# Turning rows into columns by block transposes and DRAM: a network's inner rows on ScalarE's queue, and two branches and half a convolution taken off TensorE

## Time and profile before

| | |
|---|---|
| median of 3 runs | 891.3 us |
| the profiled execution | 890.65 us, its span 888.9 us |
| mean granted clock of TensorE | 0.997 |
| TensorE, VectorE, ScalarE busy | 99%, 71%, 52% of the span |
| mean DMA rate | 242 GB/s |

### The profile page before, as it was taken

The page is one execution under the profiler, slowest core; times in us unless marked ns, Lnnn a source line. Parts: engine busy times, 40 slices in busy tenths (PEclk is TensorE's granted clock), DMA queues, the critical chain, the costliest instruction groups (busy, mean ns, idle before and its releaser), DMA issues.

```text
span 888.9 us, 11084 instructions
## 1 busy us (share of the span) xinstructions
PE 878.5 (99%) x4079; PEld 732.8 (82%) x4079; DVE 631.6 (71%) x883; ACT 460.7 (52%) x697; POOL 40.8 (5%) x66
## 2 busy tenths in 40 slices
PE   9999999999999999999999999999999999999996
PEld 7878888888998888888888888888888888888885
DVE  6769987837558877688578886875768766665743
ACT  6546554626688475446535554454445344444530
POOL 0010000022103000000000000001000100000000
PEclk9999999999999999999999999999999999999998
DMA  9899999774654454454699999975755577777741
GB/s 365 346 323 352 359 363 351 270 237 145 182 175 175 162 193 164 149 186 143 218 308 348 344 329 323 333 257 163 257 179 177 182 248 241 240 233 246 250 120 47
DMA packets 94879, 215.12 MB, mean 242 GB/s; under 512 B 14520, under 2 KB 46185, under 8 KB 94697
## 3 DMA queue, kind: packets, MB, share of 16 engines
q1 hardware_dynamic: 94104, 212.97, 69.8%
q10 hardware_dynamic: 720, 1.44, 0.4%
HBM read 204.66 MB, written 9.72 MB: 241 GB/s over the span
## 4 chain that ended last, share of the span: by engine, by line
PE 94%; DMA 2%; DVE 1%; issue 1%; ACT 1%; SPq 0%; POOL 0%; POOLq 0%; DVEq 0%
PE ps L741 29%; PE ps L743 29%; PE ps L742 29%; DMA t_raw<-in_f_up 2%; PE ps L679 1%; PE ps L656 1%; PE ps L649 1%; PE ps L858 1%; PE ps L874 1%; PE ps L816 0%; PE ps L850 0%; PE ps L798 0%; DVE t_wl L1209 0%; DMA t_acc<-in_xT 0%; PE ps L865 0%
## 5 line engine op out<-in xcount | busy, mean ns | idle before, releaser
L1209 DVE TENSOR_TENSOR t_wl<-t_raw,t_wh 128x1024 fp32r<-128x1024 f32 (+3 forms) x308 | 360.4, 1203 | 103.3 <-ACT t_wh L916 102.4
L916 ACT ACTIVATE t_wh<-t_raw 128x1024 fp32r<-128x1024 f32 (+3 forms) x308 | 307.8, 1040 | 106.9 <-DMA t_raw<-in_f_up 63.3
L741 PE MATMUL ps<-t_wh,t_XH 128*128 128x512 f32 (+2 forms) x640 | 250.2, 391 | 1.3 <-DVE t_wl L1209 1.3
L743 PE MATMUL ps<-t_wh,t_XL 128*128 128x512 f32 (+2 forms) x640 | 247.1, 386 | 0.0
L742 PE MATMUL ps<-t_wl,t_XH 128*128 128x512 f32 (+2 forms) x640 | 246.8, 386 | 0.0
L741 PEld LDWEIGHTS ps<-t_wh,t_XH 128*128 128x128 f32 x640 | 120.2, 188 | 24.8 <-DVE t_wl L1209 2.1
L743 PEld LDWEIGHTS ps<-t_wh,t_XL 128*128 128x128 f32 x640 | 120.1, 188 | 24.0
L742 PEld LDWEIGHTS ps<-t_wl,t_XH 128*128 128x128 f32 x640 | 120.3, 188 | 22.9
L741 PE MATMUL ps<-t_wh,t_YH 128*128 128x512 f32 x288 | 113.1, 393 | 0.2 <-DVE t_YL L1634 0.2
L743 PE MATMUL ps<-t_wh,t_YL 128*128 128x512 f32 x288 | 112.2, 390 | 0.0
L742 PE MATMUL ps<-t_wl,t_YH 128*128 128x512 f32 x288 | 112.2, 389 | 0.0
(11 more groups left out here) (225 smaller groups left out, 614.1 us busy)
## 6 DMA issues: line engine op xcount, KB each, us to landing
t_raw<-in_f_up SPq DMA_DIRECT2D x130, 512.0 KB, 5.6
t_raw<-in_f_dn SPq DMA_DIRECT2D x66, 512.0 KB, 5.5
t_raw<-in_ada SPq DMA_DIRECT2D x48, 512.0 KB, 6.3
inner_rows<-t_tp SPq DMA_DIRECT2D x60, 128.0 KB, 3.8
t_tp<-inner_rows SPq DMA_DIRECT2D x15, 512.0 KB, 5.2
t_raw<-in_mkv SPq DMA_DIRECT2D x8, 512.0 KB, 3.6
t_raw<-in_ga SPq DMA_DIRECT2D x8, 512.0 KB, 3.3
t_raw<-in_gc SPq DMA_DIRECT2D x8, 512.0 KB, 3.2
```

Source lines behind the costliest of these rows:

```text
L741: pe.matmul(o, xh, h, start=k == 0, stop=False)
L743: x = pe.matmul(o, xl, h, start=False, stop=k == n - 1)
L916: act.activation(wh[:, m % SPL, lo:w], raw[:, n % RAW, lo:w], ACT.Copy).then_inc(hi_made, 1)
L1209: dve.tensor_tensor(wl[:, n % RAW, lo:w], raw[:, n % RAW, lo:w], wh[:, m % SPL, lo:w].bitcast(F32), ALU.subtract).then_inc(drained, 1)
```

## The change

1. The nets' `spill` and `reload` move from SyncE's list to ScalarE's, with the same transfers. Their places are later: `ways` goes from (3, 4, 6) to (3, 5, 7) for the first of the first net, from (0, 1, 3) to (1, 2, 3) for the fifth of each net, and from (0, 1, 4) to (2, 4, 6) for the rest.
2. Branches c and a go by block transposes and DRAM (`blocks`, `spill`, `reload`, `y_in`), with SyncE's queue and two further buffers, the halves of `acc2`. Branch b keeps TensorE's way. `load_cond(1)` moves from unit 41 to 57 of the mixing block, since `cond` is one of these buffers.
3. Half 0 of the convolution goes the same way, `u` through `tp` and the gate through half of `acc2`. `cT` has four rows of 512 in place of two, so that half 0's taps stay there. Its gate product (`gate_in`) comes in the first unit of `conv_gb1`, its low parts (`gate_low` 0,0 and 0,1) in the last. Half 1 keeps TensorE's way.

```diff
-            ways = (3, 4, 6) if (f, q) == ("f1", 0) else (0, 1, 3 if q == 4 else 4)
+            ways = (3, 5, 7) if (f, q) == ("f1", 0) else (1, 2, 3) if q == 4 else (2, 4, 6)
...
+    for n, br in ((36, "c"), (39, "a")):
+        for m, step in ((0, "blocks"), (1, "spill"), (3, "reload"), (6, "y_in")):
+            side[n + m] = side.get(n + m, []) + [(step, br)]
...
-                unit("conv_cc1", m, *([("gate_turn", 0, m), ("gate_low", 0, m)] if m < 2 else []))
+                unit("conv_cc1", m, *([], [("ut_in",), ("spill", "gb")], [("conv_taps", 0, 0)], [("reload", "gb"), ("conv_taps", 0, 1)])[m])
...
-        for m, steps in enumerate(([("conv_turn", i, 0), ("conv_turn", i, 1)], [("conv_taps", i, 0)], [("conv_taps", i, 1)], [])):
+        if i == 0:
+            S.append(("blocks", "uu"))
+            turns = [], [("spill", "uu")], [], [("reload", "uu")]
+        else:
+            turns = ([("conv_turn", i, 0), ("conv_turn", i, 1), ("gate_in",)], [("conv_taps", i, 0)], [("conv_taps", i, 1)],
+                     [("gate_low", 0, 0), ("gate_low", 0, 1)])
+        for m, steps in enumerate(turns):
             unit(f"conv_gb{i}", m, *steps, ahead=5 + (i and m // 2))
         S.append(("conv_gb", i))
+        if i == 0:
+            S.append(("blocks", "gb"))
...
-            cT = sb("cT", [P, 2, 512], F32, c)
+            cT = sb("cT", [P, 4, 512], F32, c)
...
+        way = tp, acc2[:, 1, :], acc2[:, 0, :]
...
+        def way_out(q, key):
+            n, w = way_width(*key), way_of(*key)
+            q.wait_ge(*blocked.at(*key))
+            for i in range(4):
+                rows = inner_rows[w, i, :, :, 0:n // 8].rearrange("b f e -> f b e")
+                q.dma_start(rows, way[w][32 * i:32 * i + 32, 0:n].rearrange("f (b e) -> f b e", b=8)).then_inc(spilled[w], 16)
+        def way_back(q, key):
+            n, w = way_width(*key), way_of(*key)
+            q.wait_ge(*is_out(*key))
+            rows = inner_rows[w, :, :, :, 0:n // 8].rearrange("i (t j) f e -> (j f) (i t) e", t=2)
+            q.dma_start(way[w][:, 0:n].rearrange("p (b e) -> p b e", b=8), rows).then_inc(reloaded[w], 16)
...
         @block.scalar
+            def spill(*key):
+                if key[0] in FFNS:
+                    way_out(act, key)
+            def reload(*key):
+                if key[0] in FFNS:
+                    way_back(act, key)
...
+            def gate_in():
+                act.wait_ge(*cg_made.at(0, 1))
+                for j in (0, 1):
+                    gate_hi(0, j)
...
         @block.vector
+            def gate_in():
+                dve.wait_ge(*taps_made.at(0, 1))
+                dve.wait_ge(*is_back("gb"))
+                for t in (0, 1):
+                    c = parts_of(cT[:, 0:2, :].rearrange("p j (c n) -> p (j c) n", c=2), t)
+                    dve.tensor_tensor(c, placed(t, "gb"), c, ALU.mult).then_inc(*cg_made.by(0, t))
```

More of the change, by code:

```diff
@@ L517, in build @@
         inner_keys = [(f, q) for f in FFNS for q in range(6)]
-        blocked = Signal(sem("blocked"), inner_keys)
+        turned_keys = steps("blocks")
+        blocked = Signal(sem("blocked"), turned_keys)
+        spilled, reloaded = ([sem(f"{n}{w}") for w in range(3)] for n in ("spilled", "reloaded"))
         hid_hi, hid_lo = Signal(sem("hid_hi"), both(inner_keys)), Signal(sem("hid_lo"), both(inner_keys))
-        spilled, reloaded = sem("spilled"), sem("reloaded")
         halves = steps("half")
@@ L590, in out_of, with way_of, is_back, is_out @@
                             "ukv0": "kv0", "ukv1": "kv1"}.get(name, name), t)
[L592 to L606, removed]
+        def way_of(*key):
+            return {"c": 1, "a": 2, "gb": 1}.get(key[0], 0)
+        def is_back(*key):
+            w = way_of(*key)
+            mine = [k for k in turned_keys if way_of(*k) == w]
+            return reloaded[w], 16 * (mine.index(key) + 1)
+        def is_out(*key):
+            w = way_of(*key)
+            mine = [k for k in turned_keys if way_of(*k) == w]
+            return spilled[w], 64 * (mine.index(key) + 1)
+        def way_width(*key):
+            return 512 if key[0] in FFNS and key[1] == 5 else 1024
+        def way_out(q, key):
[9 more added lines that the diff above has]
+            q.dma_start(way[w][:, 0:n].rearrange("p (b e) -> p b e", b=8), rows).then_inc(reloaded[w], 16)
+        def placed(t, *key):
+            rows = way[way_of(*key)][:, 0:way_width(*key)]
+            return rows.rearrange("p (i t c n) -> p t c i n", i=4, t=2, n=32)[:, t]
+        def chunk_back(c, *key):
+            return way[way_of(*key)].rearrange("p (i t c n) -> p c t i n", i=4, t=2, n=32)[:, c]
+        def parts_of(a, t):
+            return a[:, :, t * P:t * P + P].rearrange("p c (i n) -> p c i n", i=4)
+        def inner_chunks(a, q):
+            return a[:, 4 * q:min(4 * q + 4, 22), :]
+        def by_block(rows):
+            return rows.rearrange("p (t i n) -> p t i n", t=2, i=4)
         def psum_2(bank):
@@ L1331, in hid, with blocks @@
                                                  op1=ALU.mult).then_inc(*hid_made.by(f, g, t))
-            def blocks(f, q):
-                n = inner_width(q) // 2
-                dve.wait_ge(*hid_made.at(f, 2 * q + (q < 5), 1))
-                dve.transpose(tp[:, 0:2 * n].rearrange("p (t n) -> p t n", t=2), hp[:, :, 0:n]).then_inc(*blocked.by(f, q))
+            def blocks(what, *key):
+                to = way[way_of(what, *key)]
+                if what in FFNS:
+                    q, = key
+                    n = way_width(what, q) // 2
+                    dve.wait_ge(*hid_made.at(what, 2 * q + (q < 5), 1))
+                    dve.transpose(to[:, 0:2 * n].rearrange("p (t n) -> p t n", t=2), hp[:, :, 0:n]).then_inc(*blocked.by(what, q))
+                    return
+                if what == "c":
+                    dve.wait_ge(mval, 8)
+                    rows = QM
+                elif what == "a":
+                    dve.wait_ge(ya_made, 2)
+                    rows = U
+                elif what == "uu":
+                    dve.wait_ge(*uu_made.at(0, 1))
+                    rows = UU
+                else:
+                    dve.wait_ge(*gb_made.at(0, 1))
+                    rows = GB
+                for t in (0, 1):
+                    m = dve.transpose(to[:, 512 * t:512 * t + 512].rearrange("p (j c n) -> p c j n", j=4, c=4),
+                                      rows[:, t, :].rearrange("p (c j n) -> p c j n", c=4, j=4))
+                m.then_inc(*blocked.by(what, *key))
@@ L1598, in conv_uu @@
                 if i:
-                    dve.wait_ge(turned, place["ut", 0, 1][1])
+                    dve.wait_ge(*blocked.at("uu"))
                 for t in (0, 1):
```

81 lines of the change are left out of this document (44 added, 37 removed), and 4 rows, old and new, of the table side.

## The result

The changed kernel takes **917.0 us** (median of 4 runs, 912.5 to 918.4) against 891.8 us of the kernel before on the same chip (4 runs, 890.0 to 892.4): ratio 1.029, 95% interval 1.027 to 1.030, slower. The forecast was 892.5 us with a range up to 896.5. The profiled execution took 918.40 us, its span 916.7 us, 27.75 us more than the profiled one of before.

What follows compares the result with a forecast made beforehand. The prediction took TensorE, busy 99% of the span, as the bound. Its terms: -3.5 - 1.7 + 0 + 5.2 - 0.5 + 1.7 = +1.2 us, on the median 891.3 giving 892.5 us, range 887.5 to 896.5.

Steps and rivals of the forecast that it cites:

- part 3: Nets: ScalarE's added issues and waits stay hidden by units split ahead; 0 us, bounds 0 and 5.
- Part 2: First net: SyncE no longer blocked, weight loads go on, TensorE's wait near 58 us ends; -1.7 us, between 0 and -1.7.
- With no unit ahead: Nets: a turn as slow as the first holds ScalarE, and TensorE as long, some 5 us; the upper bound.
- 11 us of cover: Nets: where splits run four or more units ahead, 11 us, ScalarE's wait costs TensorE nothing.
- Rival D: First net, fifth and sixth turns: ScalarE starves TensorE, 3 to 5 us on top, so 896 us; chance 0.15.
- sign for D: In the changed profile TensorE would wait for `t_wl` by more than 2 us in all.
- 1, transposes: Branches c and a, half 0's u and gate: 32 transposes leave TensorE's path; -3.5 us.
- 4, stall before co0: First matmul of co0 on YH: TensorE waits for VectorE's late `gate_low`; +5.2 us, bounds 4.0 and 6.5.
- 4, unit 236: Unit 236 of co0: its wait for half 1's gates ends; -0.5 us.
- 5, clock at co0: Behind the stall at co0: idle time lowers the clock; +1.7 us, between 0 and 2.7.
- mixing block's added copies: Mixing block: VectorE's added block transposes and copies replace as many others, hidden by units ahead; 0, bounds 0 to +1 us.
- The two thirds: Clock ramp at co0: share taken of the 2.7 us upper bound, giving +1.7 us, because dense matmuls follow.

Runs made afterwards that it cites:

- the versions with c seven units later: Against the changed kernel: nets by SyncE, a by TensorE, c's blocks at unit 43, copies behind attention; three placings of half 0's gate: 891.4, 888.8 and 888.2 us.
- the mended versions: Changed kernel with nets by SyncE, fifth turn at its old place, c's copies behind attention, a by TensorE, half 0's gate moved: first 892.0 us, last 888.2 us.
- early gates: Changed kernel with half 0's `gate_low` three units earlier, in the first unit of conv_gb1: median 908.2 us, ratio 1.017 without the last run.
- small `ada_w` loads: Changed kernel with only 8 of 1024 columns loaded for the first 24 tiles of `ada_w`, which stream through the first net: 903.0 us, ratio 1.010.
- halved packets: Changed kernel with each weight load made two transfers of half the width, rows of 2 KB in place of 4 KB: 908.0 us, ratio 1.021.

## Why the prediction was wrong

**The step that failed is part 3**, what ScalarE takes over: "I take 0; the bounds are 0 and 5 us". It measured 23.5 us in the profiled execution, 19.1 by the difference of medians when SyncE issues again. Two things in it were wrong.

- *The durations were read under the wrong load.* I took 3.8 and 5.2 us for write and read from the page's medians and put the slow first turn of before down to loads standing in the same queue. The loads were indeed the cause, but another queue gets past them only by turns: one small packet for each large one, 594 and 592 in 6 us. And the read of before was fast because SyncE, blocked in its wait, had let its queue run out, and the next loads stood behind the read. Part 2 counted the freed loads as a gain and part 3 kept a read time that existed only because they were not free. That is one fact used twice with opposite signs.
- *The bound was of one turn.* "With no unit ahead" gave 5 us as the end. The first turn alone cost 10.5, since a read of 15.2 us is longer than the 11 us of cover named there, and behind it, as behind the stall of 3.51 us at the fifth turn, the clock had fallen. Four places lost time, not one.

Rival D, ScalarE starving TensorE in the nets, was the right mechanism, with the first net and the fifth turns rightly among its places, held at 0.15 and priced at 3 to 5 us; the range stopped at 896.5. The prediction's own sign for D, more than 2 us of waits for `t_wl`, came out at 17.6. What was said against it, that the slow transfers stood behind loads of SyncE's own queue, was the misreading.

The sentence on the Trainium skill ("DMA: Bandwidth & Descriptors", section "Issuing engines are not separate DMA queues"), that transfers of both queues interleave on the same 16 engines and only issue time is saved, is borne out by the view of 54 to 60 us; the prediction took it as leaving the sum unchanged, when with the earlier trace rows it spoke for D.

**The other terms, one by one.**

| part | forecast | measured |
|---|---|---|
| 1, transposes | -3.5 | -3.6 |
| 2, first net's waits | -1.7 | -1.9 (then buried under the first turn); -1.2 with SyncE blocked as before |
| 4, stall before co0 | +5.2 | +5.1 |
| 4, unit 236 | -0.5 | -0.5 |
| 5, clock at co0 | +1.7 (up to 2.7) | +2.6 |
| mixing block's added copies | 0 to +1 | +2.5 |

In part 2 the size was about right and the cause given was not needed: with the nets on SyncE again, which is then blocked as before, the later places alone end the wait at 58 us. What freeing SyncE adds, the runs do not show.

In part 5 the upper bound was the right value. The two thirds were taken because TensorE would come back to dense matmuls; it did, and they ran at 1.2 GHz for 5.1 us all the same, about as long as the 5.35 us at the kernel's start.

The last row was not seen as what it is. The copies `y_in` were put down as replacing copies of the same count. They stand in the attention loop, where TensorE's next scores wait for ScalarE's exponentials by turns, and the copies of c and of a take 1.14 us of ScalarE's list each; before, c's stood ahead of that loop, at unit 31. TensorE waited there twice, for about 1 us. With c's copies behind the loop and a on TensorE again both waits are gone (the versions with c seven units later). The chain from the copies to each wait was not followed further.

Without the nets' turns the forecast would have read 892.5 + 0.9 + 2.5, 895.9, and the version with the nets on SyncE took 897.9; the remaining 2 us are its fifth turns (1.3 and 1.0 us), the price of their later places: with the fifth turn at its old places, in the mended versions, they are gone.

**Not settled.** Some kernels with both queues busy have executions far apart (901 to 919 us with early gates, 896 to 910 with small `ada_w` loads), but not all: the nets on ScalarE's queue alone lay within 3.6 us, and two of the kernels with SyncE alone in the nets spread over 4.8 and 4.9. Which turns lose differs from one profiled execution to the next, and only one of each kernel has a trace. Why is not shown; that it depends on how the loads happen to stand is a guess. The second stall pair, units 35 and 36, is the third turn's (its read took 12.4 us) by its time alone; it is missing with halved packets, but also with the nets alone on ScalarE's queue.

## What to carry to other kernels

A small-packet transfer that an engine waits for must not run beside another queue that is kept full of large packets: price it by a stretch of the trace in which the DMA engines are full, not by a median over quiet ones. When a change both frees a queue and relies on transfer times measured while that queue was blocked, only one of the two can be counted. And where two engines hand work back and forth, put an added step behind the product that the critical engine wants next: here, in the profiled executions, the same gate work cost 4.9 us ahead of `UU` and 1 us behind it.

## What the hardware showed that I had not expected

- A read of 512 KB in packets of 0.5 KB took 3.9 us behind a queue run empty, 15.2 us beside another queue full of 4 KB packets, and 11.0 us beside one full of 2 KB packets. While it passed, the two queues moved equal numbers of packets: 594 and 592, then 839 and 841. Its first packet started 3.5 and 3.6 us after the issue.
- An idle time of 5.1 us cost 2.6 us more by the clock; matmuls ran at 1.2 GHz for 5 us after it. Idle times of 8.7 and 3.5 us cost 1.8 and 3.1 us more.
- The executions of one kernel with two busy queues lay 13.5 us apart without the longest (901.0 to 914.5), against 3.6 us between 17 of the kernel before (890.1 to 893.7); but those of the kernel with the nets alone on ScalarE's queue lay within 3.6 us too.
